# A diffusion block on one Trainium2 core: the first four modulation blocks in another order, and the first product split around them

## The reference

```python
mod = jax.nn.silu(c) @ w_ada[layer] + b_ada[layer]
mod_c = jax.nn.silu(c_ctx) @ w_ada[layer] + b_ada[layer]
sh1, sc1, gt1, sh2, sc2, gt2 = jnp.split(mod[:, None, :], 6, axis=-1)
sh1c, sc1c, gt1c, sh2c, sc2c, gt2c = jnp.split(mod_c, 6, axis=-1)
h = modulate(rms_norm(x_lat, norm1_g[layer]), sh1, sc1)      # h * (1 + scale) + shift
hc = modulate(rms_norm(x_ctx, norm1_g[layer]), sh1c, sc1c)
mix, mix_c = token_mixer(h, hc, w_in[layer], ...)
```

## Time and profile before

| | |
|---|---|
| median of 3 runs | 1830.57 us (1829.31 to 1833.48) |
| the profiled execution's span, first to last instruction | 1825.3 us |
| its own time beside the span | the runs' median is 5.3 us longer than the span; no time of the profiled execution itself is listed |
| TensorE busy | 1549.9 us (85%) |
| VectorE busy | 668.0 us (37%) |
| ScalarE busy | 394.2 us (22%) |
| moved by DMA | 572.52 MB, mean 314 GB/s |

### The profile page before, as it was taken

How to read it: one execution, slowest core, us unless ns; L and a number is a source line. 1 busy time by engine, 2 the same in 40 slices (tenths; PEclk the granted TensorE clock), 3 DMA queues, 4 the chain that set the end, 5 groups by cost and what they waited for, 6 DMA issues and landing times.

```text
span 1825.3 us, 21752 instructions
## 1 busy us (share of the span) xinstructions
PE 1549.9 (85%) x8872; PEld 983.8 (54%) x8872; DVE 668.0 (37%) x1501; ACT 394.2 (22%) x710; POOL 46.5 (3%) x64
## 2 busy tenths in 40 slices
PE   6989999989999999997987777767797968676766
PEld 4544568878888877766443433334453524242433
DVE  3267566648898356676210101000222100010102
ACT  4222341011220024232221211111222211121211
POOL 0000000000110000001000000000000000000000
PEclk9999999999999999998897889888997988888888
DMA  9535854874549924215799999999987999999996
GB/s 366 198 129 184 309 204 156 305 262 176 201 168 341 351 94 172 96 59 240 320 429 427 429 429 428 429 428 428 413 348 308 430 428 429 428 428 429 428 428 290
DMA packets 110828, 572.52 MB, mean 314 GB/s; under 512 B 9188, under 2 KB 15460, under 8 KB 86184
## 3 DMA queue, kind: packets, MB, share of 16 engines
q1 hardware_dynamic: 109776, 569.79, 77.4%
q10 hardware_dynamic: 984, 1.79, 0.3%
HBM read 570.51 MB, written 1.05 MB: 313 GB/s over the span
## 4 chain that ended last, share of the span: by engine, by line
PE 59%; DMA 33%; DVE 4%; ACT 2%; SPq 1%; issue 1%; DVEq 0%; ACTq 0%
DMA ring<-in_w_exp_up_dram 32%; PE bank L494 18%; PE bank L1291 10%; PE bank L976 9%; PE bank L1005 4%; PE bank L502 2%; PE bank L1317 2%; PE bank L1371 2%; PE bank L1023 2%; PE bank L1327 1%; PE bank L1278 1%; PE bank L650 1%; DMA ring<-in_w_ada_dram 1%; PE bank L708 1%; PE bank L660 1%
## 5 line engine op out<-in xcount | busy, mean ns | idle before, releaser
L1291 PE MATMUL bank<-ring,arena 128*32 128x512 f32 x1792 | 259.4, 732 | 185.7 <-DMA ring<-in_w_exp_up_dram 183.8
L1291 PEld LDWEIGHTS bank<-ring,arena 128*32 128x32 f32 x1792 | 66.9, 131 | 374.7 <-issue 222.9
L2712 DVE COPY arena<-bank 128x256 f32<-128x256 f32 x32 | 13.6, 425 | 571.6 <-PE bank L1307 571.6
L976 PE MATMUL bank<-hT,ring 128*128 128x256 f32 x704 | 156.1, 384 | 4.2 <-ACT hT L1561 4.2
L976 PEld LDWEIGHTS bank<-hT,ring 128*128 128x128 f32 x704 | 135.3, 193 | 25.1 <-issue 6.2
L1317 PE MATMUL bank<-ring,arena 128*32 128x512 f32 x960 | 129.9, 688 | 1.9 <-DVE arena L2716 1.9
L1905 ACT COPY arena<-bank 128x512 f32<-128x512 f32 x32 | 33.4, 1045 | 432.2 <-PE bank L1291 432.2
L494 PE MATMUL bank<-ring,hT 128*128 128x512 f32 (+2 forms) x320 | 124.3, 543 | 0.0
L1327 PE MATMUL bank<-arena 128*128 128x256 f32 x512 | 119.0, 385 | 1.8 <-DVE arena L2724 1.8
L1327 PEld LDWEIGHTS bank<-arena 128*128 128x128 f32 x512 | 94.6, 190 | 41.1 <-issue 29.6
L1278 PE MATMUL bank<-arena 128*128 128x32 f32 x960 | 109.9, 274 | 0.0
(11 more groups left out here) (372 smaller groups left out, 1609.0 us busy)
## 6 DMA issues: line engine op xcount, KB each, us to landing
ring<-in_w_exp_down_dram SPq DMA_DIRECT2D x60, 2048.0 KB, 18.5
ring<-in_w_exp_gate_dram SPq DMA_DIRECT2D x56, 2048.0 KB, 19.2
ring<-in_w_exp_up_dram SPq DMA_DIRECT2D x56, 2048.0 KB, 23.7
ring<-in_w_mod_dram SPq DMA_DIRECT2D x16, 2048.0 KB, 14.5
ring<-in_w_ada_dram SPq DMA_DIRECT2D x12, 2048.0 KB, 13.8
ring<-in_w_up_dram SPq DMA_DIRECT2D x10, 2048.0 KB, 11.5
ring<-in_w_in_dram SPq DMA_DIRECT2D x8, 2048.0 KB, 14.2
arena<-in_w_mod_dram SPq DMA_DIRECT2D x8, 2048.0 KB, 8.2
```

What stands on the lines that cost most here:

```text
L976: ins = pe.matmul(b[:, 0:T], x[:, k, j * 128:j * 128 + 128], hT[:, k, 0:T], start=(k == 0), stop=(k == KD - 1))
L1291: ins = pe.matmul(bank[0][32 * q:32 * q + 32, :], xe[:, k * CAP:(k + 1) * CAP], xs[q // 2][:, o:o + 512], start=(k == 0), stop=(k == KD - ...
```

## The change

The first four blocks are loaded and multiplied in the order 2, 0, 3, 1 (`FIRST_MODS`): scale and shift of the low features, then scale and shift of the high ones. The product's weights `kvr` are loaded between the second and the third of them, and `qc` now stands ahead of `w_ukv`. The first product is cut into four parts (`low_rank_in(quarter, half)`), over the slices 0 to 3 or 4 to 7 and the tokens of one half. The two parts over the low slices run around the third block's product, the two others behind everything. Its four banks come from the second ring. VectorE and ScalarE scale and shift in the same quarters; a semaphore `shift_ready` tells ScalarE that the sums of the last block are there. The number of matmuls, of scaled and of shifted slices, and of bytes loaded is the same; the gains are four instructions on 4 columns instead of two on 8.

```diff
--- before.py
+++ after.py
@@ -36,7 +36,8 @@
 
 SUMMED = list(range(4, 12)) + list(range(16, 36))
 BESIDE = list(range(16, 24))
-ROWS_ORDER = [0, 1, 2, 3, "g0", 12, 13, 14, 15, "g1", "g2", "g3", "g4", "g5", "g6"]
+FIRST_MODS = (2, 0, 3, 1)
+ROWS_ORDER = [*FIRST_MODS, "g0", 12, 13, 14, 15, "g1", "g2", "g3", "g4", "g5", "g6"]
 SUM_SLOTS = 7
 MLA_FILL = {0: ("gk", 0), 3: ("gk", 1), 5: ("gk", 2), 7: ("gk", 3), 9: ("gv", 0), 11: ("gv", 1), 13: ("gv", 2),
             15: ("gv", 3)}
@@ -201,13 +202,14 @@
         src = w["w_ada"][0] if i < 12 else w["w_mod_2"][0] if i < 24 else w["w_mod_2"][1]
         cols(("mod", i), src, (i % 12) * 512, 512)
 
-    mods = iter(range(36))
-    for _ in range(4):
-        mod(next(mods))
+    mods = iter(range(4, 36))
     w_in = w["w_in"][0]
-    cols("kvr", w_in, IN_KV, IN_GQ - IN_KV)
+    for i in FIRST_MODS:
+        mod(i)
+        if i == FIRST_MODS[1]:
+            cols("kvr", w_in, IN_KV, IN_GQ - IN_KV)
+    cols("qc", w_in, 0, Q_LORA)
     cols("w_ukv", w["w_ukv"][0], 0, 1024, 2)
-    cols("qc", w_in, 0, Q_LORA)
     cols("w_uq", w["w_uq"][0], 0, MLA_H * QH, 3)
     for j in range(MLA_H):
         mod(next(mods))
@@ -689,26 +691,34 @@
                 b = G.open(pe, ("xt", k))
                 turn(("xt", k), b, [x_tm[:, tb, k * 128:k * 128 + 128] for tb in range(4)])
             pe.wait_ge(sem("cond_ready"), 4)
-            mod(0)
+            mod(FIRST_MODS[0])
             norm(0, second=True)
-            mod(1)
+            mod(FIRST_MODS[1])
             norm(1, second=True)
-            mod(2)
-            mod(3)
             mod_turn()
 
 
-            x = w3(weights(pe, "kvr"), KD, 288)
-            for half in range(2):
-                bs = [G.open(pe, ("kvr", 2 * half + t)) for t in range(2)]
-                for k in range(KD):
-                    normed(half, k + 1)
-                    for t in range(2):
-                        tb = 2 * half + t
-                        ins = pe.matmul(bs[t][:, 0:288], hT[:, k, tb * 128:tb * 128 + 128], x[:, k, 0:288],
+            x_kvr = w3(weights(pe, "kvr"), KD, 288)
+            bs_kvr = [G.open(pe, ("kvr", tb), second=True) for tb in range(4)]
+
+            def low_rank_in(quarter, half):
+
+                for i in range(4):
+                    k = 4 * quarter + i
+                    pe.wait_ge(sem("normed"), 8 * quarter + 4 * half + i + 1)
+                    for tb in (2 * half, 2 * half + 1):
+                        ins = pe.matmul(bs_kvr[tb][:, 0:288], hT[:, k, tb * 128:tb * 128 + 128], x_kvr[:, k, 0:288],
                                         start=(k == 0), stop=(k == KD - 1))
                         if k == KD - 1:
                             G.close(ins, ("kvr", tb))
+
+            low_rank_in(0, 0)
+            mod(FIRST_MODS[2])
+            low_rank_in(0, 1)
+            mod(FIRST_MODS[3])
+            mod_turn()
+            for half in range(2):
+                low_rank_in(1, half)
             G.over("kvr")
             x = w3(weights(pe, "qc"), KD, Q_LORA)
             for tb in range(TB):
@@ -1556,14 +1566,18 @@
 
             def shift(c, by, dst):
 
-                for k in range(KD):
-                    act.wait_ge(sem("scaled"), KD * (c - (c > 6)) + k + 1)
+                shift_part(KD * (c - (c > 6)), by, dst, 0, KD)
+
+            def shift_part(before, by, dst, lo, hi):
+
+                for k in range(lo, hi):
+                    act.wait_ge(sem("scaled"), before + k - lo + 1)
                     act.activation(dst[:, k, :], dst[:, k, :], ACT.Identity, bias=by[:, k:k + 1]).then_inc(sem("normed"), 1)
 
             def mod(i):
 
                 b = G.take(act, ("mod", i))
-                if i:
+                if i != ROWS_ORDER[0]:
                     act.wait_ge(done, G.number[("mod_t", ROWS_ORDER[ROWS_ORDER.index(i) - 1])])
                 G.give(act.activation(mrow, b, ACT.Copy), ("mod", i))
 
@@ -1580,15 +1594,20 @@
             for k in range(KD):
                 G.read(act, ("xt", k))
             squares(0, xT)
-            mod(0)
+            mod(FIRST_MODS[0])
             root(0)
             squares(1, xcT)
-            mod(1)
+            mod(FIRST_MODS[1])
             root(1)
-            mod(2)
-            mod(3)
-            shift(0, mc(0, 0), hT[:, :, 0:T])
-            shift(1, mc(0, 0, 1), hT[:, :, T:2 * T])
+            for quarter in range(2):
+                if quarter:
+                    mod(FIRST_MODS[3])
+                    act.wait_ge(sem("shift_ready"), 1)
+                for half in range(2):
+                    shift_part(8 * quarter + 4 * half, mc(0, 0, half), hT[:, :, half * T:half * T + T], 4 * quarter,
+                               4 * quarter + 4)
+                    if quarter + half == 0:
+                        mod(FIRST_MODS[2])
 
             def rms_root(tag, tb, n, dim, at_):
 
@@ -2039,18 +2058,30 @@
                 b = G.take(dve, ("xt", k))
                 dve.tensor_copy(xT[:, k, :], b[:, 0:T])
                 G.give(dve.tensor_copy(xcT[:, k, :], b[:, T:2 * T]), ("xt", k))
-            mod(0)
+            def set_gain_part(quarter):
+                for half in range(2):
+                    link(dve.scalar_tensor_tensor(gains(half)[:, 4 * quarter:4 * quarter + 4], mc(0, 1, half, 4 * quarter, 4), 1.0,
+                                                  vc("norm1_g", 4 * quarter, 4), ALU.add, ALU.mult))
+
+            def norm_part(quarter):
+                for half, src in enumerate((xT, xcT)):
+                    for k in range(4 * quarter, 4 * quarter + 4):
+                        dve.scalar_tensor_tensor(hT[:, k, half * T:half * T + T], src[:, k, :], gains(half)[:, k:k + 1],
+                                                 rs_ctx if half else rs, ALU.mult, ALU.mult).then_inc(sem("scaled"), 1)
+
+            mod(FIRST_MODS[0])
+            set_gain_part(0)
             for k in range(1, KD, 2):
                 G.read(dve, ("xt", k))
             invert(0)
-            mod(1)
             invert(1)
-            mod(2)
-            mod(3)
-            set_gain(0, mc(0, 1), vc("norm1_g", 0, KD))
-            set_gain(1, mc(0, 1, 1), vc("norm1_g", 0, KD))
-            norm(0, xT, gains(0), hT[:, :, 0:T])
-            norm(1, xcT, gains(1), hT[:, :, T:2 * T])
+            mod(FIRST_MODS[1])
+            norm_part(0)
+            mod(FIRST_MODS[2])
+            set_gain_part(1)
+            norm_part(1)
+            mod(FIRST_MODS[3])
+            dve.sem_inc(sem("shift_ready"), 1)
 
 
             def low_rank(tag, tb, to, n, at_, say):
```

## The result

The changed kernel takes 1835.39 us (median of 20 runs, 1831.84 to 1837.86) against 1830.29 us for the kernel before (median of 20, 1825.25 to 1834.02). The ratio is 1.0029, 95% interval 1.0022 to 1.0036: 5.1 us more, and the whole interval lies above the 0.2% that I had named as the edge. The forecast was 1835.8, between 1831.5 and 1838.5.

The account below looks back on a forecast made before the run. TensorE was taken to bound the kernel after the fourth block's load; the first product's end moving from 56.52 to 61.75 (+5.2) made the span 1830.5, plus 5.3 from span to median: 1835.8 us, range 1831.5 to 1838.5.

Parts of the forecast that it names:

- Only the first product's end counts, and its shift passes to the end: Any shift of the first product's end, 56.52 us before, carries one to one to the kernel's end.
- Loads: First four blocks and product weights, reordered, land by about 36.0 us, each before TensorE needs it; no cost.
- Start of the first quarter: First product starts at 32.0 us, 7.1 earlier than before, set by the context's reciprocal on VectorE.
- The block between the quarters: Scale high's product, ScalarE's copy and shift and a hand-over before the second quarter cost 3.2 us.
- The last relay: From shift high's product to the high half: 7.95 us, its sums queued behind eight scaled slices on VectorE.
- The clock: Two long TensorE waits each bring a half-clock stretch, at the first quarter and the high half; 1.4 us each.
- The sum: First product ends at 61.75 instead of 56.52, +5.2 us; span 1830.5 plus 5.3 gives 1835.8 us.
- The order pays: Rival: the kernel gets faster, 4.7 us earlier at 1825.9, if TensorE reaches shift high when it lands; chance 0.08.
- Three slow bursts: Rival: the second quarter of the product also runs at the slow clock; +6.6 us, 1837.2; chance 0.04.
- Hidden later: Rival: the experts' loads absorb the shift of the product's end, leaving 1830.6 us; chance 0.04.
- The one with waits that leave the clock alone: Rival: no clock fall in the new waits gives +2.4 us, 1833.0; one fall +3.8, 1834.4; under +3.7: 0.28.

Follow-up runs that it names:

- e2: Changed kernel with ScalarE's context shifts of the low half ahead of its copy of the third block's row; 1839.35, 1835.37 and 1837.17 us in three timings.
- e4: Kernel before with only its loads reordered, the product's weights between the second and third block; 1833.65 us, 1.0018.
- e1: Changed kernel with VectorE's sums for the last block behind the first of the eight high-half slices instead of behind all eight; 1832.68 us, 1.0016.
- e3: Changed kernel with six extra products, which change nothing in the result, in each of TensorE's two long waits; 1832.05 us, 1.0014.
- e7: Kernel before with nine extra products, whose result nobody reads, in TensorE's waits around the fourth block's product; 1828.58 us, 0.9989.
- after_again: The changed kernel, unaltered, timed once more as the base of a later round; 1835.56 us, 1.0031 to the kernel before.
- e5: Changed kernel with TensorE's order altered: third block ahead of the first quarter, last turn inside the second quarter; 1826.51 us, 0.998 to the kernel before.
- e8: e5 with five extra products in the wait ahead of the third block; 1825.10 us, 0.9972 to the kernel before.

## Why the prediction came out right, step by step

- **Only the first product's end counts, and its shift passes to the end.** Held: +7.0 at the product's end, +7.1 at 111.16. The experts' first load on the chain ended at 943.29 + 33.31 = 976.60 instead of 931.75 + 36.80 = 968.55, +8.1, and the span +8.7. On the way the shift was not constant: 7.9 at 128 us of the kernel before, 6.6 at 450, 6.8 at 828, 8.2 at 884. No single stretch makes the extra 1.0 to 1.7. Between 828 and 833 the shift grew by 1.0, in part by a turn that took 0.87 us where it took 0.45 before. So "one to one" held to within 1.7 us. No load absorbed the shift, and the table's third column ranks the kernels as the times do, apart from e2 and from pairs whose intervals overlap.
- **Loads.** They landed ahead of every use, as said; e4 shows what the same order costs where the last block does gate.
- **Start of the first quarter.** 32.0 foretold, 31.42 measured in an execution whose first block began 0.60 earlier. The relay over the context's reciprocal was right to 0.1 us.
- **The block between the quarters.** 3.2 foretold, 41.48 - 38.52 = 2.96. ScalarE's shift behind the copy cost 0.40 where I had taken the 0.52 of one that starts from rest.
- **The last relay.** 7.95 foretold, 53.14 - 45.63 = 7.51, for a like reason: behind the slices the sums need no hand-over. Its cause was the one named, the eight slices in VectorE's queue; e1 took 2.5 of it away by order alone.
- **The clock.** That both long waits make it fall was right, and e3 and e7 show that the waits are the cause. The term was mis-sized. I allowed 1.4 for each. Against the full-clock lengths of e3 (4.15 and 8.03) the losses were 2.95 and 2.35 in the first profile, 1.66 and 2.11 in the second. I had capped one at 1.7 from the single stretch of 3.41 us in the earlier trace rows. That fits the first quarter of `after_again`, where the clock was at 0.50 from about 33.8 to 37.1. The other three stretches lasted some 6.8 us. They began inside the wait, so part of each fell on no work, and still the matmuls lost 2.1 to 3.0.
- **The sum.** 32.0 + 5.35 + 3.2 + 3.95 + 7.95 + 9.3 = 61.75 became 31.42 + 7.10 + 2.96 + 4.15 + 7.51 + 10.38 = 63.52. In the times the change is +5.1, as forecast (+5.2). The agreement of the total is partly luck. The relays were put 0.7 too long and the clock's losses 1.0 to 2.5 too small; the pace was 0.5 too quick in all (4.15 and 8.03 at the full clock for 3.95 and 7.9). And the profile of before, to which all this was added, was 3 us quicker than its median: I took the 5.3 between its span and the median for a fixed amount, of which only 2.1 is. The profiles put the product's end later by 7.6 or 6.1, counted from the first block, where the medians differ by 5.1.
- **The rivals.** "The order pays" failed where it was said to, at the time when TensorE reaches the last block: 45.6, not under 37.0. e5 shows that the idea itself was sound. The same order of loads and the same four parts gain 3.3 us once the third block fills the early wait and the slices are done before the last turn. "Three slow bursts" did not occur: the second quarter ran at 1.00 in every profile of the changed kernel. "Hidden later" did not either. The one with waits that leave the clock alone fell with the two stretches at 0.50, and e3 confirmed it.

The Trainium skill's rule that I had weighed ("TensorE: Matmul & The Clock Gate", "HAM oscillation — how this bites in real kernels") speaks of bursts that are shorter than the waits between them. None of the three bursts here is: at the full clock they take 4.15, 4.15 and 8.03 us, behind waits of 3.56, 1.11 and 3.60. So I stretched it when I took it for all three, and these bursts neither bear it out nor contradict it; two of them began slow although they are longer than their waits.

What stays open: why e2's medians lie above the changed kernel's when its product ends earlier and its profiled executions are not slower; and what decides whether the clock is low for some 3.4 us behind a long wait or for 6.8.

## What to carry to other kernels

When a product is split to start earlier, write down for each engine what stands ahead of the last part's inputs in its list. Here the gain was there, and it was given back because eight slices that nobody needed yet stood ahead of two small sums, and because a block product lay between the parts instead of in the wait before them. And count a wait of TensorE at more than its length: in this kernel the waits of 3.0 to 3.6 us around the first product cost another 1.7 to 3 us in the matmuls behind them, and extra products that change nothing took that back.

## What the runs showed of the hardware

- The clock can stay at half for some 6.8 us although TensorE works nearly all that time: 30.81 to 37.45, with 6.03 us of work in 6.64. Behind the same wait of 3.56 us it stayed there for 3.4 us in `after_again`, and likewise behind one of 3.04 (e5, 32.46 to 35.83).
- The length of a wait alone does not tell: in the kernel before, one of 2.57 us (until 33.03) left the clock at 1.00, and in one of 2.58 (until 117.68), with one of 1.39 ending four us earlier, it fell to 0.50.
- The clock also fell behind two short waits with a turn between them, 0.84 and 1.08 us around 0.6 us of work (e1, at 51.00), where a single wait of 1.1 us ahead of the second quarter did not.
- Products with zero weights, or into a bank that is overwritten later, keep the clock at 1.00 (e3, e7, e8), so the result need not be used.
- A small part that no edit touched took 1.95 us in one execution and 3.64 in another (the four records of line 936, `after_again` and the third e2), by the clock that it met.
